# A decoder step with 64 experts: half of the expert pairs get their token rows from a 0/1 matmul, the others through VectorE turns, and the last pair is taken expert by expert

## The chip, the cores and the metric

The kernel runs on one core of one Trainium2 chip, in fp32. The metric is the device time of one execution in microseconds (us). Before the change three executions took 932.84, 932.85 and 930.03 us, a median of 932.84.

## The reference, cut to what matters

One inference step of a one-layer decoder for 256 prompt tokens and 8 sample tokens, model width 1024. A mixer (latent attention beside a state-space branch) comes first; the change does not touch its arithmetic. Then a mixture of experts:

```python
scores = sigmoid(t @ w_router)                 # t: 264 tokens x 1024, 64 experts in 8 groups
...                                            # the best 4 groups, in them the best 6 experts
combine = ...                                  # (264, 64): a token's weight for an expert, else 0
gte = einsum('td,edf->tef', t, w_gate_e)       # 64 experts, 1024 -> 256
upe = einsum('td,edf->tef', t, w_up_e)
routed = einsum('tef,efd->td', silu(gte) * upe * combine[:, :, None], w_down_e)
shared = (silu(t @ w_gate_s) * (t @ w_up_s)) @ w_down_s
out = x + g2 * rms_norm(routed + shared)
```

Each expert has 2 MiB of gate and up weights and 1 MiB of down weights, 192 MiB for all 64, and each weight is read once.

## The kernel before, in words

**Experts in pairs.** Experts are taken in 32 pairs q (experts 2q and 2q+1). For every pair a tile of 128 places is filled: four blocks of 32 places, one for each expert of the pair and each half of the prompt (l = 0: tokens 0 to 127, l = 1: tokens 128 to 255). In a block, LS = 28 places are for chosen prompt tokens and the last 4 hold sample tokens, which all experts compute. What does not fit into 28 places goes through a loop at the end (not entered with these inputs as long as no block overflows).

**Where the rows come from.** The normalised rows `h2` (two tiles of 128 tokens, also kept turned as `h2t`) are stored to DRAM as `tok_rows`. The router's choice is turned into a table `tab_g` of token numbers by four rounds of max and match_replace on VectorE (`take_lists`) and 8 small matmuls on TensorE (L2045). For each pair GpSimd issues `gather` (L1826), an indirect DMA from `tok_rows` into one of two buffers `xg`, and `gather_weights` (L1899), an indirect DMA of the routing weights into `wv` from `weight_tab`, a copy of the weights in DRAM (L1922). TensorE turns the 128 rows with 8 transposes (`turn_rows`, L2062), ScalarE copies them out of PSUM into `xt` (`rows_half`, L2331), and `xt` is the stationary operand of the expert's products.

**One pair on TensorE.** In this order: `gate_up(2q)`, `gate_up(2q+1)` (L2148, 32 instructions each; an fp32 product is two instructions); the two halves of `down_half(q-1, h)` (L2086), `turn_rows(q+1)`, `turn_inner(q)` (L2158, turns the inner activations), `combine` of pair q-1 (L2097, a matmul with a 128x128 weight matrix `wmat` that adds a pair's rows to the tokens' sums in PSUM banks 0 to 3). Between them ScalarE does the silu (L2342), VectorE multiplies gate and up (`hh`, L2571), makes `wmat` (L2535), copies the two halves of `down` out of PSUM (`half_out`, L2526), copies the turned inner activations (L2579) and adds the sample rows (`add_own`, L2562).

**Weights.** SyncE's queue loads gate/up weights into 6 slots and down weights into 6 slots. `load_gu(e)` waits until `gate_up(e-6)` is done; `load_dn(e)` waits until the pair's `down` before it in that slot is done. The down weights of the last two pairs come in two column halves (`load_dn_halves`, L1821). Expert 4's gate/up slot is the place of the shared expert's weights, so it is loaded in four parts, each when a part of the shared product is done (L1854); after the last of them the queue loads down weights 5 and 6 (L1814, L1861).

**The start of the stage.** TensorE does the last mixer product, the router (L1977) and the shared expert's gate and up products (`shared`, L1984), with the turns of `key` (L2033) and the table matmuls between them. The first `gate_up` starts after all of that.

**The end.** After `combine` of expert 63, ScalarE squares and VectorE scales the rows, each half when its sums are done; ScalarE loads the table for Sqrt once, at L2357, after its last silu. Then the rows are stored.

## Time and profile before

| | |
|---|---|
| median of the runs | 932.84 us |
| the profiled execution, its own time | 932.54 us |
| its span, first to last instruction | 930.8 us |
| PE busy | 870.0 us, 93% |
| DVE, ACT, POOL busy | 353.6, 194.6, 128.7 us |
| moved by DMA | 324.72 MB, mean 349 GB/s |

The span is cut into stretches below. In a row of windows the columns are: the stretch, its length, the busy time (and instructions) of PE, PEld, DVE, ACT and POOL, the granted TensorE clock as a share of full speed, the share of time in which the 16 DMA engines were busy, and the rate in GB/s. In a row of the timeline they are start, length, engine, line, operation, what is written and read, the shape, how many instructions are merged, and in brackets the idle time before it and what ended it. A row of groups ends with busy time, mean length of one instruction in ns, and idle time before them. The expert stage runs from about 453 us to 921 us.

### The profile page before, as it was taken

Reading aid. Unit: us, or ns where it says so; the run is one execution under the profiler, and the core shown is the slowest. Engines: PE = TensorE matmul, PEld = TensorE weight load, DVE = VectorE, ACT = ScalarE, POOL = GpSimd, SP = SyncE. Lnnn points to the kernel's source line nnn. Section 1 sums busy time; section 2 is a strip of 40 time slices with the busy share of each in tenths; the row PEclk is TensorE's granted clock in tenths of the full one; section 3 lists DMA queues with packets and bytes.
Section 4 is the critical chain, followed back from the end, with each engine's and each line's share of the span. In section 5 each row is a group of like instructions: output and inputs, shape, how many; then the busy total and the mean of one; then the engine's idle time right before and its main releaser. Section 6 shows DMA issues by size and latency. Waiting matters only on the chain.

```text
span 930.8 us, 18059 instructions
## 1 busy us (share of the span) xinstructions
PE 870.0 (93%) x7470; PEld 564.3 (61%) x7470; DVE 353.6 (38%) x800; ACT 194.6 (21%) x506; POOL 128.7 (14%) x155
## 2 busy tenths in 40 slices
PE   5999999997889899899899999999999998989897
PEld 3788888875666677657755555554555554545452
DVE  2315580037344689336223322322233222222225
ACT  2000110316222398033111111111111110101012
POOL 0000000022476000000302211101011110101100
PEclk9999999999999999999999999999999999999998
DMA  9966766727499939999999999999999999999993
GB/s 367 398 225 245 283 256 239 301 91 264 151 339 340 383 120 321 384 419 385 362 422 418 423 418 423 418 422 422 416 424 418 422 419 422 420 424 419 423 373 134
DMA packets 58564, 324.72 MB, mean 349 GB/s; under 512 B 13849, under 2 KB 22922, under 8 KB 37938
## 3 DMA queue, kind: packets, MB, share of 16 engines
q1 hardware_dynamic: 47154, 305.43, 81.8%
q0 software_dynamic: 9568, 17.93, 5.6%
q8 instruction: 61, 1.00, 0.4%
q10 hardware_dynamic: 1760, 0.20, 0.2%
q14 instruction: 21, 0.17, 0.1%
HBM read 326.55 MB, written 7.45 MB: 359 GB/s over the span
## 4 chain that ended last, share of the span: by engine, by line
PE 42%; DMA 17%; SPq 2%; DVE 2%; ACT 1%; issue 1%; POOLq 0%; DVEq 0%; ACTq 0%
PE bank L2148 17%; PE bank L2086 9%; PE bank L2097 4%; DMA slot_b<-in_w_e 4%; DMA x<-in_w_e 4%; DMA row_of<-in_w_e 4%; PE bank L1955 3%; PE bank L2062 2%; SPq L1806 1%; DMA ring<-in_w_units 1%; DMA out_ssm_s<-st 1%; DMA ac<-x_row 1%; PE bank L2158 1%; PE bank L2132 1%; SPq L1814 1%
## 5 line engine op out<-in xcount | busy, mean ns | idle before, releaser
L423 PE MATMUL bank<-h,ring 128*128 128x264 f32 x608 | 138.4, 388 | 0.5 <-PE bank L423 0.3
L423 PEld LDWEIGHTS bank<-h,ring 128*128 128x128 f32 x608 | 114.6, 190 | 21.9 <-issue 2.6
L2571 DVE TENSOR_TENSOR con<-scales_of,bank 64x256 f32<-64x256 f32 x64 | 27.2, 425 | 236.7 <-ACT scales_of L2342 236.7
L1826 POOL DMA_INDIRECT xg<-tok_rows,tab_g x32 | 36.1, 1129 | 364.4 <-PE bank L2062 315.1
L2086 PE MATMUL bank<-ring,ht 128*32 128x512 f32 x320 | 72.5, 595 | 10.1 <-DMA x<-in_w_e 5.2
L2342 ACT ACTIVATE scales_of<-bank 64x256 f32<-64x256 f32 x64 | 24.2, 378 | 274.0 <-PE bank L2148 274.0
L2148 PE MATMUL bank<-done_out,xt 128*64 128x256 f32 x704 | 78.4, 381 | 0.1
L2148 PE MATMUL bank<-ring,xt 128*64 128x256 f32 x672 | 77.2, 382 | 0.4 <-ACT xt L2331 0.4
L2526 DVE COPY sq<-bank 128x512 f32<-128x512 f32 x64 | 44.3, 692 | 73.5 <-PE bank L2086 73.5
L2148 PEld LDWEIGHTS bank<-done_out,xt 128*64 128x64 f32 x704 | 50.5, 137 | 30.1 <-issue 7.0
L2148 PEld LDWEIGHTS bank<-ring,xt 128*64 128x64 f32 x672 | 46.8, 137 | 35.0 <-issue 14.1
L2097 PE MATMUL bank<-sq,con 64*128 64x512 f32 x256 | 65.6, 609 | 0.0
L2331 ACT COPY xt<-bank 128x448 f32<-128x448 f32 x64 | 31.0, 532 | 134.3 <-PE bank L2062 134.3
L2086 PEld LDWEIGHTS bank<-ring,ht 128*32 128x32 f32 x320 | 18.2, 109 | 52.8 <-issue 52.8
L2062 PEld LDWEIGHTS bank<-con,xg 128*128 128x128 f32 x256 | 27.4, 140 | 27.5 <-issue 27.5
L637 POOL DMA_DIRECT2D page<-in_cache x20 | 12.0, 601 | 231.6 <-issue 224.3
L2086 PE MATMUL bank<-done_out,ht 128*32 128x512 f32 x176 | 39.9, 595 | 4.4 <-DMA row_of<-in_w_e 4.4
L2148 PE MATMUL bank<-slot_b,xt 128*64 128x256 f32 x352 | 39.9, 379 | 0.8 <-DMA slot_b<-in_w_e 0.8
L2086 PE MATMUL bank<-slot_b,ht 128*32 128x512 f32 x176 | 39.9, 595 | 0.0
L2086 PE MATMUL bank<-row_of,ht 128*32 128x512 f32 x176 | 39.9, 595 | 0.0
L2562 DVE SCALAR_TENSOR_TENSOR acc<-sq,own_w,acc 128x1024 f32<-128x1024 f32 x30 | 38.3, 1275 | 0.0
L2062 PE MATMUL bank<-con,xg 128*128 128x128 f32 x256 | 34.9, 279 | 1.8 <-DVE con L2571 1.0
(471 smaller groups left out, 1281.2 us busy)
## 6 DMA issues: line engine op xcount, KB each, us to landing
ring<-in_w_units SPq DMA_DIRECT2D x25, 2048.0 KB, 11.4
done_out<-in_w_e SPq DMA_DIRECT2D x22, 2048.0 KB, 29.5
ring<-in_w_e SPq DMA_DIRECT2D x20, 2048.0 KB, 28.7
slot_b<-in_w_e SPq DMA_DIRECT2D x11, 2048.0 KB, 30.5
slot_f<-in_w_e SPq DMA_DIRECT2D x10, 2048.0 KB, 29.8
ring<-in_w_e SPq DMA_DIRECT2D x19, 1024.0 KB, 30.8
slot_b<-in_w_e SPq DMA_DIRECT2D x10, 1024.0 KB, 30.2
done_out<-in_w_e SPq DMA_DIRECT2D x10, 1024.0 KB, 28.7
```

Source lines behind the costliest of these rows:

```text
L423: mm = pe.matmul(bank[:, t % NB, 0:T], w[:, j, k, :], h[:, k, :], start=(k == 0), stop=(k == KD - 1))
L1826: pool.indirect_dma_start(xg[q % AHEAD][:, :], None, tok_rows, bass.IndirectOffsetOnAxis(ap=tab_g[:, q:q + 1].bitcast(U32), axis=0), bound ...
L1955: mm = pe.matmul(bank[:, 2 * j + h, :], merged[:, k, j * P:(j + 1) * P], w_out[:, k, part_of(h)], start=(k == 0), stop=(k == KD - 1))
L2062: mm = pe.transpose(bank[:, 5 + h, i * P:(i + 1) * P], xg[q % AHEAD][:, k * P:(k + 1) * P], ident)
L2086: mm = pe.matmul(bank[lo:lo + HB, 6 + h, :], ht[q % 2][:, e % 2 * 2 + k, l * HB:(l + 1) * HB], down_at(e)[:, k, h * 512:(h + 1) * 512], st ...
L2097: mm = pe.matmul(bank[:, 2 * l + h, :], wmat[q % 2][at, :], yo[q % NYO][at, h * 512:(h + 1) * 512], start=(q == 0), stop=(q == NPAIR - 1))
L2148: mm = pe.matmul(bank[c * LB:(c + 1) * LB, 4 + e % 2, 0:FE], xt[:, k, e % 2 * LB:(e % 2 + 1) * LB], gu_w[e % SLOTS][:, k, c * FE:(c + 1) * ...
L2331: act.copy(xt[:, KD // 2 * h:KD // 2 * (h + 1), :].rearrange("p k (x s) -> p k x s", s=HB)[:, :, :, 0:LS], bank[:, 5 + h, :].rearrange("p ...
L2342: act.activation(sg[e % 2][:, :], bank[0:LB, 4 + e % 2, 0:FE], ACT.Silu).then_inc(sg_ready, 1)
L2526: dve.tensor_copy(yo[q % NYO][:, h * 512:(h + 1) * 512], bank[:, 6 + h, :]).then_inc(y_ready, 1)
L2562: ins = dve.scalar_tensor_tensor(acc[:, :], yo[q % NYO], own_w[:, q:q + 1], acc[:, :], ALU.mult, ALU.add)
L2571: dve.tensor_tensor(hh[e % 2][:, :], sg[e % 2][:, :], bank[LB:2 * LB, 4 + e % 2, 0:FE], ALU.mult).then_inc(hh_ready, 1)
```

## The change

1. `gather` serves only every second pair of pairs (q mod 4 = 2 or 3, called fetched), into a single buffer `xg`. GpSimd issues them in its loop: for q mod 4 = 0 after the weights of q the rows of q+2, for q mod 4 = 2 ahead of the weights of q the rows of q+1. VectorE turns them (`turn_rows`): for each expert of the pair 8 transposes of 32 partitions x 256 elements straight from `xg` into `xt`.
2. For q mod 4 = 0 or 1, four experts at a time (a group, EG = 4), TensorE forms `xt` with `burst`: 16 matmuls of `h2` (128x128, stationary) with a 0/1 matrix `sel` (128 x 4x28 columns), which selects and turns at once; ScalarE copies four results (`take_rows`). `sel` comes from a count of chosen tokens ahead of each (a matmul with `before`, `pos_done`), `places` and `select` on VectorE. `h2` now has a place of its own.
3. `half_out` moves from VectorE to ScalarE.
4. The start: the bursts of group 0, the two `pos` matmuls and 8 transposes of the sample rows come before the second half of the shared products; the lists (`keys_of`, `take_lists`) and the table matmuls come after them. The sample rows go into `xg` by four small DMAs.
5. Gate/up weights of expert 5: the last 2560 of 4096 columns are loaded in the mixer's last phase, the rest as before.
6. The end: only the last pair's down weights come in column halves; expert 63's gate/up weights come last but these, in two halves; TensorE does `gate_up(62)`, `down` and `combine` of pair 30, and then `gate_up(63)`.

```diff
@@ the mixer's last phase, SyncE
                         load_row(0)
                         load_row(1)
+                        sp.dma_start(slot_f[:, EARLY_GU:GU], io["w_e"][5][:, EARLY_GU:GU]
+                                     ).then_inc(small_in, 16)
                         sp.wait_ge(y_done6, 2)
@@ SyncE, expert stage
-                        sp.wait_ge(own_in, 1)
+                        sp.wait_ge(own_cols, 2)
                         load_dn(sp, 5)
-                        sp.wait_ge(rows_stored, 32)
+                        sp.wait_ge(wgt_ready, 1)
                         sp.dma_start(w_sd[:, :, :].rearrange("p k c -> p (k c)"), io["w_e"][EXTRA][:, GU:EW]).then_inc(w_sd_in, 16)
                         for e in range(NE):
-                            if e + SLOTS < NE:
+                            last = e + SLOTS == NE - 1
+                            if e + SLOTS < NE and not last:
                                 load_gu(sp, e + SLOTS)
-                            if e % 2 and 3 <= e < NE - 7:
+                            if e % 2 and 3 <= e < NE - 5:
                                 for n in (e + 3, e + 4):
-                                    if EXTRA < n < NE - 4:
+                                    if EXTRA < n < NE - 2:
                                         load_dn(sp, n)
+                            if last:
+                                sp.wait_ge(gu_done, e + 1)
+                                for h in range(2):
+                                    part = slice(h * GU // 2, (h + 1) * GU // 2)
+                                    sp.dma_start(gu_at[(NE - 1) % SLOTS][:, part], io["w_e"][NE - 1][:, part]).then_inc((gu_in[(NE - 1) % SLOTS], last_gu_in)[h], 16)
                             if e == NE - 6:
-                                load_dn_halves(sp, NE - 4)
-                            if e == NE - 5:
                                 load_dn_halves(sp, NE - 2)
@@ GpSimd
+                        pool.wait_ge(srow_took, 1)
+                        for x4 in range(4):
+                            pool.dma_start(xg[x4 * HB + LS:(x4 + 1) * HB, :], rows_s[x4 % 2 * OWN:x4 % 2 * OWN + OWN, :]).then_inc(own_in, 16)
                         pool.wait_ge(wgt_ready, 1)
                         for a, lo in ((0, 0), (2, P)):
                             pool.dma_start(weight_tab[lo * NE:(lo + P) * NE, :].rearrange("(t e) o -> t (e o)", e=NE),
                                            wgt[:, a, :]).then_inc(tab_stored, 16)
-                        gather(pool, AHEAD)
+                        pool.wait_ge(own_in, 16 * 4)
+                        pool.wait_ge(rows_stored, 32)
                         pool.wait_ge(tab_stored, 32)
-                        gather_weights(0)
-                        gather_weights(1)
-                        gather(pool, AHEAD + 1)
-                        for q in range(2, NPAIR):
-                            if q + AHEAD < NPAIR:
-                                gather(pool, q + AHEAD)
+                        for q in range(NPAIR):
+                            if q % 4 == 2:
+                                gather(pool, q + 1)
                             gather_weights(q)
+                            if q % 4 == 0:
+                                gather(pool, q + 2)
@@ TensorE
+                        def burst(n, i):
+                            l, ks = i // 2, range(KD // 2 * (i % 2), KD // 2 * (i % 2 + 1))
+                            ...
+                            for k in ks:
+                                at = k % (KD // 2) * P
+                                out = bank[:, b, at:at + P].rearrange("p (e s) -> p e s", e=EG)[:, :, 0:LS]
+                                mm = pe.matmul(out, h2[:, l, k * P:(k + 1) * P], sel[:, l, :, :], start=True, stop=True)
+                            mm.then_inc(xt_done, 1)
@@ TensorE, start of the stage (order after the change)
                         shared(0, 0, 0, P)
                         shared(0, 0, P, T - P, low)
+                        pe.wait_ge(chosen_ready, 1)
+                        pe.matmul(bank[:, 1, 0:NE], ccol("before"), chosen[:, 0, :], start=True, stop=True).then_inc(pos_done, 1)
+                        shared(0, 0, P, T - P, high).then_inc(sgu_done, 1)
+                        shared(1, 0, 0, P, high)
+                        ...                                  # the same for chosen[:, 2, :]
+                        shared(1, 0, P, T - P).then_inc(sgu_done, 1)
+                        for i in range(4):
+                            burst(0, i)
                         ...                                  # key turns, shared(0, 1), shared(1, 1) first part, table matmuls
@@ TensorE, loop
-                            if q + 1 < NPAIR:
-                                for h in range(2):
-                                    turn_rows(q + 1, h)
-                            turn_inner(q)
+                            if q % 4 == 3 and q + 1 < NPAIR:
+                                for i in range(4):
+                                    burst((q + 1) // 4, i)
+                            if q < NPAIR - 1:
+                                turn_inner(q)
@@ VectorE
-                        def half_out(n):
+                        def turn_rows(q, h):
+                            if h == 0:
+                                dve.wait_ge(x_in, 16 * (nth_fetched(q) + 1))
+                            dve.wait_ge(gu_done, 2 * q - 3 + h)
+                            for l in range(2):
+                                at = h * LB + l * HB
+                                rows = xg[at:at + HB, :].rearrange("p (k r c) -> p r k c", k=KD, r=4)
+                                for r in range(4):
+                                    ins = dve.transpose(xt[32 * r:32 * r + 32, :, 2 * q % EG + h, l, :], rows[:, r, :, :])
+                            ins.then_inc(turned_ready, 1)
                         for q in range(NPAIR):
                             for e in (2 * q, 2 * q + 1):
+                                if e == NE - 1:
+                                    weight_matrix(q - 1)
                                 ...                          # wait for the silu, multiply: hh
+                                if q % 4 == 1 and e % 2 == 0:
+                                    turn_rows(q + 1, 1)
+                                if q % 4 == 2:
+                                    turn_rows(q + 1, e % 2)
-                            if q:
+                            if q and q < NPAIR - 1:
                                 weight_matrix(q - 1)
-                                half_out(2 * q - 2)
-                                half_out(2 * q - 1)
                             ...                              # wait for turn_inner, copy ht, add_own(q - 1)
+                            if q % 4 == 0:
+                                turn_rows(q + 2, 0)
+                            if q % 4 == 1 and q + 3 < NPAIR:
+                                dve.wait_ge(xt_done, q + 3)
+                                select(slice(0, 2), q // 2 + 2).then_inc(sel_ready, 1)
                             if q == 0:
                                 own_weights()
```

TensorE waits at q = 1, between the two halves of `down` of pair 0, for what `own_weights` writes; that wait is in both kernels.

## Rows read from the trace of the kernel before

**Rows 1.** Windows: whole core, five stretches.
```profile
344.00:348.00 4.00, 4.00 (x53) 3.52 (x52) 2.12 (x3) 3.97 (x14) 0.00 (x0) 1.00 0.00 0
448.00:452.00 4.00, 3.24 (x29) 3.07 (x28) 0.43 (x1) 0.00 (x0) 0.36 (x1) 1.00 0.77 263
500.00:550.00 50.00, 50.00 (x440) 26.54 (x434) 16.17 (x27) 6.14 (x14) 10.69 (x8) 1.00 1.01 421
...
913.00:916.00 3.00, 3.00 (x27) 1.25 (x20) 1.97 (x4) 0.00 (x0) 0.00 (x0) 1.00 0.16 59
916.00:919.00 3.00, 3.00 (x28) 0.81 (x28) 1.60 (x4) 0.00 (x0) 0.00 (x0) 1.00 0.06 16
```

**Rows 2.** The chain that ended last: turns, a shared product, one pair, waits, the end.
```profile
474.21 1.02 PE bank L2062 x8
...
630.76 3.63 PE bank L2132 x8
...
707.09 7.06 PE bank L2148 x64
714.14 3.57 PE bank L2086 x32
717.71 1.02 PE bank L2062 x8
718.74 0.33 PE bank L2158 x3
719.07 1.83 PE bank L2097 x8
...
796.08 37.95 DMA row_of<-in_w_e
...
858.18 38.60 DMA x<-in_w_e
...
921.32 0.70 DVE slot_b L2665
```

**Rows 3.** DMA issues, 880 to 931 us, and SyncE's timeline: the last halves.
```profile
row_of<-in_w_e SPq DMA_DIRECT2D x2, 512.0 KB, 11.1
...
906.08 1.16 SPq L1821 DMA_DIRECT2D row_of<-in_w_e  x1
```

**Rows 4.** Timeline of TensorE at the start of the stage.
```profile
443.31 0.33 PE L2045 MATMUL bank<-con,listed_p 128*32 128x32 f32 x16 [0.95 <-DVE listed_p L2475]
443.57 7.55 PE L1984 MATMUL bank<-x,ring 128*128 128x128 f32 x64
451.88 1.07 PE L2062 MATMUL bank<-con,xg 128*128 128x128 f32 x8 [0.76 <-DMA xg<-tok_rows,tab_g]
453.30 3.03 PE L2148 MATMUL bank<-ring,xt 128*64 128x256 f32 x26 [0.35 <-ACT xt L2331]
```

**Rows 5.** DMA queues, 500 to 700 us: packets, MB, share of 16 engines.
```profile
q0 software_dynamic: 2386, 2.80, 4.0%
```

**Rows 6.** VectorE's timeline: the last step of the routing weights.
```profile
446.27 0.58 DVE L2511 TENSOR_SCALAR wgt<-wgt,need 128x64 f32<-128x64 f32 x3
```

**Rows 7.** GpSimd's timeline: a gather behind the turns that free its buffer.
```profile
476.00 0.99 POOL L1826 DMA_INDIRECT xg<-tok_rows,tab_g  x1 [11.73 <-PE bank L2062]
```

**Rows 8.** DMA issues, 445 to 470 us: size, median us to landing.
```profile
weight_tab<-wgt POOLq DMA_DIRECT2D x2, 32.0 KB, 5.1
```

**Rows 9.** The gathers (L1826): landing after issue, min, median, max.
```profile
DMA to landing us min/median/max: 6.9/10.4/11.6
```

**Rows 10.** Groups of VectorE by shape; the last is from the mixer.
```profile
L2571 DVE TENSOR_TENSOR con<-scales_of,bank 64x256 f32<-64x256 f32 x61 | 25.9, 425 | 223.6 <-ACT scales_of L2342 223.6
L2535 DVE TENSOR_SCALAR con<-mod,tok_f,wv 128x128 f32<-128x128 f32 x30 | 10.2, 339 | 0.0
...
L501 DVE TENSOR_SCALAR h<-sq,scales_of,mod 128x256 f32<-128x256 f32 x8 | 2.9, 410 | 0.1
```

**Rows 11.** ScalarE's timeline: the table for Sqrt.
```profile
911.36 1.28 ACT L2357 ACT_TABLE_LOAD   x1
```

More of the change, by code:

```diff
@@ L75 @@
 SPREAD = 4
+EG = 4
 TAKEN, SENT = -3e38, 3e38
@@ L2015, in _ @@
                         turn_half(0, 1)
+                        pe.wait_ge(x1_ready, 2)
+                        for k in range(KD):
+                            mm = pe.transpose(bank[0:TS, k // 4, k % 4 * P:(k % 4 + 1) * P], h2t[:, k, TP:T], ident)
+                        mm.then_inc(srow_done, 1)
                         pe.wait_ge(score_ready, 2)
@@ L2161, in _ @@
                         pe.wait_ge(fresh, 1)
[L2162 to L2163 removed]
                         for q in range(NPAIR):
[L2165 to L2166 removed]
+                            gate_up(2 * q)
+                            if q < NPAIR - 1:
+                                gate_up(2 * q + 1)
                             if q:
@@ L2197, in _ @@
                                 more = overflow(pe)
+                        gate_up(NE - 1)
+                        turn_inner(NPAIR - 1)
                         for h in range(2):
@@ L2493, in _ @@
                         route(2, 2, 3)
+                        for l, a in ((0, 0), (1, 2)):
+                            places(l, a)
+                            select(slice(l, l + 1), 0).then_inc(sel_ready, 1)
+                        keys_of(0)
+                        keys_of(2)
                         take_lists()
```

266 lines of the change are left out of this document (151 added, 115 removed).

## The prediction, made blind

> **What bounds the kernel now.** I read the page first (PE busy 93%), then the windows, then the chain of waits, and last the timelines around the start and the end of the expert stage. The page alone misleads. In the expert stage TensorE is busy without a gap at 500 to 550 us, but the DMA share is 1.01 at 421 GB/s in the same stretch [rows 1]: two resources are full at once. The chain says which of them ends last. A pair costs TensorE 7.06 (gate and up) + 3.57 (down) + 1.02 (turn of the rows) + 0.33 (turn of the inner activations) + 1.83 (combine) = 13.81 us, and up to about 730 us the chain is nothing but this pattern. Behind it come waits for down weights that were issued 38 us earlier: they land at 796.08 + 37.95 = 834.0 and 858.18 + 38.60 = 896.8, four pairs apart, which is 15.7 us a pair [rows 2]. So TensorE (13.8) is faster than the DMA (15.7); it eats the six prefetched experts up to 730 us and then waits. The stage is bound by DMA from its start: 201 MB of expert weights, plus what else is in the queues. After 896.8 the chain is pure TensorE until 921.3, when VectorE begins the final rows; the very last weights land at 906.08 + 11.1 = 917.2 [rows 2, 3].
>
> There is one hole in the DMA: 0.77 at 448 to 452 [rows 1]. By then every free slot is filled, and what SyncE has left (a quarter of expert 4, down weights 5 and 6) waits for the last shared product, which ends at 443.57 + 7.55 = 451.1 [rows 4]. Everything after this point is one full queue of work, so the last landing moves with (a) the time at which that product ends and (b) the bytes behind it. A saving on TensorE by itself is worth nothing.
>
> **The change, part by part.** The sum is made against the profiled execution's 932.54 us (span 930.8), which is 0.3 us under the median of 932.84.
>
> *Start, TensorE.* Ahead of the last shared product come the bursts of group 0: 16 matmuls, two instructions each. The nearest price is the shared product's 7.55/64 = 0.118 us with the same 128x128 stationary operand and 128 columns [rows 4]; the burst has 112 columns. 32 x 0.118 = 3.8. The two counts add 4 instructions, 0.5. The wait of 0.95 for the lists [rows 4] goes: the lists now run beside half of the shared product (32 instructions, 3.8 us). The 8 sample-row turns cost between 0 and 0.9; I take 0.1, for ScalarE's copies are waited for there anyway. Net 3.4: the last shared product ends at 454.5. The first gate_up can start at once, where before 0.76 + 1.07 + 0.35 lay between [rows 4], so it starts at 454.5 instead of 453.3.
>
> *Start, DMA.* SyncE's last quarter, down 5 and 6 move by the same +3.4. The 1.31 MB of expert 5 that now go out at 344 to 348, where the DMA stands at 0.00 [rows 1], cost nothing there, and bring nothing either: they are taken from the stretch ahead of the hole and only make the hole 3.1 us longer. What would be hidden is hidden already.
>
> *Fewer gathers.* q0 takes 4.0% of 200 us = 8.0 us for the 200/13.81 = 14.5 pairs of that stretch, 0.55 a pair, nearly all of it the rows (2.80 MB) [rows 5]. As a mean over engines a gather is then worth 0.5. But the last landing is that of the most laden engine: after 913 us only 16% and 6% of the engines still work, for some 4 to 5 us [rows 1]. Spread over 30 gathers that is 0.15 more each. I take 0.63, bounds 0.5 and 0.8. Before, 30 gathers lay behind the hole (the first two in it), now 16: 14 x 0.63 = -8.8 (7.0 to 11.2).
>
> *Early stall.* This is the part that the change adds unawares. Routing weights: tables at 452.5, then 443.57 to 446.85, 3.3 us, as before [rows 4, 6]: 455.8. GpSimd wakes 0.8 us later, as behind the turns that end at 474.21 + 1.02 = 475.2 [rows 2], whose gather starts at 476.0 [rows 7], and stores the weights in two issues: landed at 5.1 [rows 8] plus about 2 for the fuller queues (a gather lands in 6.9 at the least and 10.4 at the median [rows 9]), 464.5. Then the weights of pair 0 (1.3), and only then the rows of pair 2 at 466, landing 10.4 later [rows 9]: 476.4. VectorE's instruction that waits for them stands ahead of own_weights, and TensorE, done with gates 0 to 3 and half a down at 472.5, waits for that. A turn for one expert is 8 transposes of 256 elements. No transpose is in the trace; the nearest are VectorE instructions of 256 elements a partition, mean 410 ns, but 8 of them busy 2.9 us in pairs, so that the second of a pair adds 0.33 [rows 10]. I take 0.33, 2.67 a turn; bounds 0.28 and 0.45 (no overlap at all). Own weights at 479.6, the next multiply (0.43), a turn, a multiply: combine of pair 0 ends near 485.5. The rows of pair 3 are issued when that turn has freed the only buffer (482.7 + 0.8 + 10.4 = 493.9) and are followed by turn, multiply, turn, wmat (0.34) [rows 10]: 500.0. TensorE reaches gate_up(6) at 501.8, some 10 us later than before. The slots freed late leave the DMA queues dry two or three times by about half a us: +1.5 (0 to 6).
>
> *Steady state, TensorE.* Without turns 12.79 a pair, a burst (3.8) every fourth: 54.96 per four instead of 55.24. No gain, and none needed. VectorE gives up half_out and gains 42.7 us of turns; it stays under half busy. But at q mod 4 = 2 it does turn, multiply, turn, wmat in a row behind a gather that was issued only when the turn before it was done. Counted from the start of q = 4: that turn ends at 20.0, rows at 20.0 + 0.8 + 10.4 = 31.2, wmat at 37.3; TensorE would like it at 36.5. So 0.75 of stall for each of 7 such pairs, 5.2 in all.
>
> *TensorE's own path.* 501.8 + 16.6 (q = 3 with burst) + 27 x 12.79 + 6 x 3.8 + two shared products (3.63 each [rows 2]) + 1.5 of small ones + 5.2 = 900.6 for gate_up(62).
>
> *DMA's path.* Last landing 917.2 + 3.4 + 1.5 - 8.8 - 0.3 (half as many narrow packets) = 913.0. Behind the down weights of expert 61 lie 4.2 MB, 10.2 us, so those land at 902.8.
>
> *End.* From 902.8: down 3.57, combine 1.83, gate_up(63) 3.53, silu and multiply 1.0, turn 0.33, copy 0.5, down 3.57, first combine 1.0: 918.1. TensorE's path gives 900.6 + 3.53 + the same 15.3 = 919.4. The split transfers are then not what ends last; expert 63's serial chain is. I take 918.8 against 921.3: -2.5. Last, half_out of expert 63 on ScalarE now stands ahead of the table load of 1.28 us, which before lay 10 us ahead of the end [rows 11]: the first square comes 1.0 later. Sum: 932.54 - 2.5 + 1.0 = 931.0.
>
> **A rule that speaks against it.** By the Trainium skill, "VectorE: DVE Perf Modes", section "The DRAIN you can't avoid", the next VectorE instruction does not start before the pipe of the last is empty; by this a turn would be 8 full lengths. The rows of 256 elements show an overlap instead (8 x 0.41 = 3.3, busy 2.9), so the trace agrees with this rule of the Trainium skill only in part. The same page of the Trainium skill, section "The three transpose paths", has 311 ns for a 128x128 bf16 turn; my estimate from it, with 128 more elements at one a cycle of 0.96 GHz, is 0.44 us an instruction; the sum by either would be that of the second rival below.
>
> **The rivals.**
>
> *The stall is hidden.* Landing under 10 us or turns of 0.30, so that VectorE is in time, gathers worth 0.7 or more: the DMA path alone with 14 x 0.75 and no early idle. Last landing 910, end 915.3, time 927.5. For it: the DMA share is 1.01 everywhere behind the hole. Against it: 10.4 is the median.
>
> *VectorE becomes the bound (slower).* Per group three turns are in the loop, 24 transposes; each 0.1 us more in one is 2.4 us per group, 17 over seven. TensorE's path has nothing to spare, so that it decides from about 0.36 us an instruction. At 0.42 (as the mean of 0.41 without overlap [rows 10]): gate_up(62) at 900.6 + 15 + 2, end 936, time 950; at 0.38, 940. Against it: single-source instructions overlap in pairs here.
>
> *The start costs more.* Weight table and rows of pair 2 land 3 us later than I took, or the chains of selects hold the bursts: both paths +4, time 935.
>
> *The change doesn't do what it says:* a block that overflows in one way of filling and not in the other would show in the loop at the end; the same 28 places are filled, so I give it nothing.
>
> **How the numbers follow.** Likeliest (0.50): both paths near each other, 931.0, own range 927.5 to 934.5. Hidden stall 0.20, VectorE as the bound 0.20, costlier start 0.10. A difference of 0.3%, 2.8 us, is what a measurement of this kernel can tell: below 930.0 is faster, above 935.6 slower. Faster: 0.24 of the first case and all of the second, 0.44. Slower: all of VectorE's case, 0.04 of the costlier start and 0.02 of the first, 0.26. Same 0.30. Range 925.5 to 941.
>
> **What would show it.** Right: the last shared product ends near 454.5; TensorE idles 5 to 8 us at L2086 or its like in pair 0's down, near 472 to 480, for own_weights; q0's share in the stage falls to nearly half; transposes 0.33 us apart; waits for down weights come late, after 850, and are short; the table load stands behind the last copies. Wrong: DMA share clearly under 1 after 500 us, waits of TensorE for w_ready in every fourth pair of more than 1 us, or a last landing after 917.

## The result: 3.4% slower

The changed kernel takes 962.84 us (median of 6, 960.72 to 965.01), the kernel before 931.37 us (median of 6); ratio 1.0341, 95% interval 1.0322 to 1.0360. The forecast was 931.0 us with a range up to 941; the time lies outside it, above even the figure that the rival "VectorE becomes the bound" gave for 0.42 us a transpose (950).

Profile after, by groups (line, engine, operation, out<-in, shape, count | busy us, mean ns | idle before it and what ended it); the last two rows are transfers of expert weights (count, size, median us from issue to landing):

```profile
L2617 DVE STREAM_TRANSPOSE xt<-xg 32x256 f32<-32x256 f32 x256 | 111.5, 436 | 29.1 <-DMA xg<-tok_rows,tab_g 25.4
L2137 PE MATMUL bank<-sq,con 64*128 64x512 f32 x256 | 76.4, 706 | 23.0 <-DVE con L2627 23.0
...
done_out<-in_w_e SPq DMA_DIRECT2D x21, 2048.0 KB, 11.4
slot_f<-in_w_e SPq DMA_DIRECT2D x9, 2048.0 KB, 10.3
```

A "turn" here is the 8 transposes of one expert's rows on VectorE; "the matrix" is `wmat`, the weights that `combine` multiplies by. A transpose lasts 436 ns, where the forecast took 330 for each. TensorE's combine (L2137) waits 23.0 us in all for the matrix from VectorE (L2627), which stands behind the turns. The expert weights now land some 9 to 13 us after their issue (medians of the tiles, 500 to 900 us), where before they took up to 38 [rows 2]: the queues are no longer backlogged. None of TensorE's waits after 440 us is for weights, so the DMA has ceased to be what sets the pace. The busy share hides this, for it hardly fell. The same 400 us before and after, us, busy time and count of PE, PEld, DVE, ACT, POOL; PE's granted clock; DMA share; GB/s:

```profile
500.00:900.00 400.00, 384.73 (x3212) 204.87 (x3208) 112.89 (x193) 46.55 (x108) 58.11 (x54) 1.00 1.01 419
500.00:900.00 400.00, 376.98 (x3058) 199.86 (x3056) 157.16 (x336) 63.38 (x129) 43.17 (x39) 0.96 0.99 411
```

VectorE at q mod 4 = 2, once in every group of four pairs (start, us, instruction, count, idle before it):

```profile
739.42 3.58 DVE L2617 STREAM_TRANSPOSE xt<-xg 32x256 f32<-32x256 f32 x8 [3.03 <-DMA xg<-tok_rows,tab_g]
743.03 0.42 DVE L2663 TENSOR_TENSOR con<-scales_of,bank 64x256 f32<-64x256 f32 x1
743.48 3.59 DVE L2617 STREAM_TRANSPOSE xt<-xg 32x256 f32<-32x256 f32 x8
747.11 0.35 DVE L2627 TENSOR_SCALAR con<-mod,tok_f,wv 128x128 f32<-128x128 f32 x1
```

A turn is 3.58 / 8 = 0.447 us from start to start: each transpose waits for the whole of the one before. TensorE at the same time:

```profile
743.51 0.46 PE L2203 MATMUL bank<-con 64*128 64x64 f32 x4 [0.98 <-DVE con L2663]
747.60 3.78 PE L2137 MATMUL bank<-sq,con 64*128 64x512 f32 x8 [3.63 <-DVE con L2627]
751.32 7.31 PE L2193 MATMUL bank<-done_out,xt 128*64 128x256 f32 x64
```

It waits 0.98 us for the multiply behind the first turn, 3.63 us for the matrix behind the second, and then the combine takes 3.78 us where it took 1.83 [rows 2]. The windows, in the same columns as above, say why:

```profile
744.00:748.00 4.00, 0.40 (x2) 0.43 (x4) 3.85 (x10) 0.00 (x0) 0.00 (x0) 0.61 0.94 401
748.00:750.00 2.00, 2.00 (x6) 0.83 (x6) 1.10 (x1) 0.00 (x0) 1.75 (x1) 0.50 1.11 475
750.00:752.00 2.00, 2.00 (x10) 0.45 (x8) 0.00 (x0) 0.00 (x0) 0.00 (x0) 0.57 0.92 393
752.00:756.00 4.00, 4.00 (x40) 2.64 (x38) 0.37 (x1) 0.38 (x1) 0.00 (x0) 1.00 1.01 414
```

Granted clock 0.50 is 1.2 GHz, the lower of its two levels; TensorE had been busy for 0.40 of the four us before. And in the chain of work that ended last the loop can be followed round (start, us, what):

```profile
781.90 3.63 PE bank L2193 x32
...
785.96 0.42 DVE con L2663
...
786.42 0.43 DVE xt L2617
...
790.78 11.43 DMA xg<-tok_rows,tab_g
...
802.23 0.43 DVE xt L2617
...
809.92 0.36 DVE con L2627
...
810.42 3.79 PE bank L2137 x8
```

These are the first gate_up of q mod 4 = 1, its multiply (after ScalarE's silu, left out here), a turn (which frees the one buffer), the next gather of 11.4 us, a turn, a multiply, a turn, the matrix, and the late combine. From the multiply to the matrix's end it is 24.3 us (785.96 to 810.28), and TensorE has work for 19.8 of them:

```profile
785.96:810.28 24.32, 19.82 (x172) 9.42 (x168) 14.70 (x33) 3.47 (x7) 1.99 (x2) 0.99 1.01 425
```

From one late combine to the next, seven groups of four pairs take 433.1 us (498.62 to 931.72), 61.9 in the mean and 59.5 to 62.8 where no shared product lies between. In the version below whose turns are on TensorE, which hardly waits, a group takes 57.0 (a gate_up at 799.16, the same of the next group at 856.12).

### The profile page after: what moved, and what is told of

Same layout as the page of the kernel before. It is cut to its first block, busy times and chain, and to the rows that moved or that the text cites. A ratio compares the mean times of both kernels' runs of the same rounds, so it can differ in the third digit from the quotient of the medians.

```text
span 963.4 us, 18257 instructions
## 1 busy us (share of the span) xinstructions
PE 885.8 (92%) x7482; PEld 568.3 (59%) x7482; DVE 423.8 (44%) x1002; ACT 218.7 (23%) x539; POOL 115.2 (12%) x140
## 4 chain that ended last, share of the span: by engine, by line
PE 39%; DMA 8%; DVE 8%; issue 3%; ACT 0%; POOL 0%; POOLq 0%; DVEq 0%
PE bank L2193 16%; DMA xg<-tok_rows,tab_g 8%; PE bank L2126 7%; PE bank L2137 6%; DVE xt L2617 6%; PE bank L2017 3%; PE bank L1976 3%; PE bank L2024 1%; DVE con L2663 1%; PE bank L2172 1%; PE bank L2203 1%; DMA weight_tab<-wgt 0%; DVE con L2627 0%; PE bank L2032 0%; PE bank L1998 0%
## 5 line engine op out<-in xcount | busy, mean ns | idle before, releaser
L2617 DVE STREAM_TRANSPOSE xt<-xg 32x256 f32<-32x256 f32 x256 | 111.5, 436 | 29.1 <-DMA xg<-tok_rows,tab_g 25.4
L2137 PE MATMUL bank<-sq,con 64*128 64x512 f32 x256 | 76.4, 706 | 23.0 <-DVE con L2627 23.0
L2126 PE MATMUL bank<-ring,ht 128*32 128x512 f32 x320 | 74.5, 607 | 6.9 <-DVE own_w L2644 6.9
L2193 PE MATMUL bank<-ring,xt 128*64 128x256 f32 x672 | 79.4, 390 | 0.0
L1923 POOL DMA_INDIRECT wv<-weight_tab,tok_i x32 | 38.0, 1186 | 318.1 <-DVE con L2627 266.5
L2395 ACT COPY sq<-bank 128x512 f32<-128x512 f32 x64 | 37.4, 585 | 94.9 <-PE bank L2126 94.9
L2137 PEld LDWEIGHTS bank<-sq,con 64*128 64x128 f32 x256 | 29.3, 213 | 41.7 <-issue 40.8
L2673 DVE COPY ht<-bank 128x256 f32<-128x256 f32 x32 | 13.6, 424 | 83.8 <-PE bank L2203 83.6
## 6 DMA issues: line engine op xcount, KB each, us to landing
done_out<-in_w_e SPq DMA_DIRECT2D x21, 2048.0 KB, 11.4
```

The lines of the kernel that those rows point to most:

```text
L1923: pool.indirect_dma_start(wv[:, q:q + 1], None, weight_tab, bass.IndirectOffsetOnAxis(ap=tab_w[:, q:q + 1].bitcast(U32), axis=0), bounds_c ...
L2126: mm = pe.matmul(bank[lo:lo + HB, 6 + h, :], ht[q % 2][:, e % 2 * 2 + k, l * HB:(l + 1) * HB], down_at(e)[:, k, h * 512:(h + 1) * 512], st ...
L2137: mm = pe.matmul(bank[:, 2 * l + h, :], wmat[q % 2][at, :], yo[q % NYO][at, h * 512:(h + 1) * 512], start=(q == 0), stop=(q == NPAIR - 1))
L2193: mm = pe.matmul(bank[c * LB:(c + 1) * LB, 4 + e % 2, 0:FE], xt[:, k, e % EG, :, :].rearrange("p l n -> p (l n)"), gu_w[e % SLOTS][:, k, c ...
L2395: act.copy(yo[q % NYO][:, h * 512:(h + 1) * 512], bank[:, 6 + h, :]).then_inc(y_ready, 1)
L2617: ins = dve.transpose(xt[32 * r:32 * r + 32, :, 2 * q % EG + h, l, :], rows[:, r, :, :])
```

## The experiments

Ratios are to the kernel before, run on the same chip; its medians there were 930.2 to 931.1 us. All edits are to the changed kernel unless said. Versions that leave out transposes, or put copies or other rows in their place, compute another product; they are there for their time.

### Fewer transposes a turn: 4, 6, 7

The first edit shortens a turn and leaves everything else in place.

```
-                                for r in range(4):
+                                for r in range(3):        # turns6; 2 in turns4; 4 if l else 3 in turns7
```

> The changed kernel with 6 of the 8 transposes of each turn (a quarter of the fetched rows is not turned, so those experts work on old columns). A turn then takes 6 x 0.447 = 2.7 us, which is what the prediction took for a whole turn. Theory (a transpose is priced wrong, the rest of the prediction holds): 931 to 936. Rival A (something else in the change costs the 30 us: the selecting matmuls, the copies on ScalarE, the order at the end): 950 or more, at most 10 us regained. Rival B (a stall also lowers TensorE's clock, so that the loss is more than the loop's excess): the gain per group is more than 6 x 0.447 = 2.7 us, and granted clock returns to 1.00 in the stage.

> 4 of the 8 transposes of each turn (half of the fetched rows not turned), a turn of 1.8 us. Theory: VectorE is out of the path and the DMA or TensorE's plain sum sets the time, 927 to 932, at most 4 us under the kernel with 6. Rival A (the turns are not it): over 945. If the loss were in proportion to the transposes all the way (no threshold), this would be as far under the kernel with 6 as that is under the changed one.

> The changed kernel with 7 of the 8 transposes of each turn (an eighth of the fetched rows is not turned): a turn of 3.13 us, as if a transpose took 0.39. By the formula of the prediction's rival (VectorE in the path from 0.36 us a transpose on, 2.4 us per group for each 0.1 us) 943. If the step from 6 to 8 transposes (930 to 963) is even, 946. If it sets in only between 7 and 8: under 935.

| transposes a turn | us a turn | median us | ratio, 95% interval |
|---|---|---|---|
| 4 | 1.8 | 928.85 | 0.9981 (0.9957 to 1.0004) |
| 6 | 2.7 | 930.21 | 1.0011 (0.9991 to 1.0031) |
| 7 | 3.1 | 946.91 | 1.0174 (1.0148 to 1.0199) |
| 8 | 3.6 | 962.84 | 1.0341 (1.0322 to 1.0360) |

With a turn of the length that the forecast took, the whole rest of the change costs what the forecast said: 930.2 against 931.0. That it agrees to 1 us is partly luck, as terms of the sum were off in both directions (below). But nothing else in the change makes it slow. Between 4 and 6 almost nothing happens (1.4 us), from 6 on each further transpose costs 16 to 17 us: a threshold, where the loop on VectorE becomes longer than TensorE's work. In the kernel with 6, TensorE's wait for the matrix is 1.45, 1.83 and 1.38 us in the first three groups and 0.16 to 0.86 from then on (7.3 in all, where the changed kernel has 23.0), and no late combine is slowed:

```profile
553.31 1.99 PE L2137 MATMUL bank<-sq,con 64*128 64x512 f32 x8 [1.83 <-DVE con L2627]
672.93 1.99 PE L2137 MATMUL bank<-sq,con 64*128 64x512 f32 x8 [0.16 <-DVE con L2627]
```

### The turns of the fetched pairs on TensorE (pe_turns)

TensorE turns the fetched rows and ScalarE copies them into `xt`, as before the change; all else stays.

```
+    for i in range(KD // 2):                     # PE: behind the down halves, banks 5 and 6, as before the change
+        k = KD // 2 * h + i
+        mm = pe.transpose(bank[:, 5 + h, i * P:(i + 1) * P], xg[:, k * P:(k + 1) * P], ident)
...
+    act.copy(xt[:, KD // 2 * h:KD // 2 * (h + 1), at:at + 2, :, 0:LS].rearrange("p k e l s -> p k (e l) s"),      # ACT
+             bank[:, 5 + h, :].rearrange("p (k x s) -> p k x s", x=4, s=HB)[:, :, :, 0:LS])
...
-    ins = dve.transpose(xt[32 * r:32 * r + 32, :, 2 * q % EG + h, l, :], rows[:, r, :, :])
```

> The changed kernel with the fetched pairs' rows turned by TensorE (8 transposes, 1.02 us a pair) and copied by ScalarE, as before the change; all else stays. TensorE's sum for four pairs becomes 4 x 12.79 + 3.8 + 2 x 1.02 = 57.0 against 55.2 before, still under the DMA's 4 x 15.7 less two gathers. Theory (VectorE's turns alone cost the time; the rest of the change is worth a little): 927 to 932. Rival A (the rest costs too): 935 to 950. Rival C (TensorE is now the bound): 932 to 936, with waits for down weights gone from the chain.

931.16 us (928.16 to 936.88), ratio 1.0019 (0.9989 to 1.0049): the loss is gone as far as can be measured, with the same number of gathers and bursts. The theory's time holds. So does the half of rival C that speaks of the profile, that TensorE is now the bound: in the profiled execution TensorE waited 2.6 us in all between 440 and 920 us (who waited for what, us in total, times, longest), and no weights are among it:

```profile
PE bank L2215 <- DVE con L2676: 1.9, 2, 0.9
PE bank L2138 <- DVE ht L2682: 0.5, 1, 0.5
PE bank L2029 <- DMA xg<-tok_rows,tab_g: 0.2, 1, 0.2
```

### A second buffer for the fetched rows (twobuf)

The rows of pairs with q mod 4 = 3 go into a place of their own (half of `h2`, whose other half the later bursts then read twice), so their gather need not wait for a turn.

```
-                pool.indirect_dma_start(xg[:, :], None, tok_rows,
+                pool.indirect_dma_start((xg[:, :], h2[:, 1, :])[q % 2], None, tok_rows,
-                    pool.wait_ge(turned_ready, 2 * nth_fetched(q))
+                    pool.wait_ge(turned_ready, 2 * nth_fetched(q) - 2)     # for the third fetched pair and on
```

> The changed kernel with all 8 transposes of 0.44 us a turn, but with a second buffer for the rows of the pairs with q mod 4 = 3, so that their gather does not wait for the turns of the pair before and lands early. (The buffer is the second half of h2; the bursts behind group 0 read its first half twice, and the sample rows are not put into it, so those values are other than the reference's.) Theory (what costs is the loop turn, gather of 10 to 11 us, turn, turn, matrix on a single buffer; VectorE's busy time is under half): VectorE starts the turns right behind its multiplies, a turn of 3.6 us still makes the second multiply and the matrix up to 1.3 us late, time 928 to 936. Rival (the turns' busy time itself, ahead of the multiplies in the queue of VectorE, is the cost): over 945.

936.78 us (934.91 to 942.09), ratio 1.0068 (1.0047 to 1.0088). All 8 transposes at full length are in it, and 26 of the 31 us are gone: busy time on VectorE by itself costs at most what is left. The rest is the loop that the single buffer closes: a gather of 11 us that can't start before a turn has ended, with two turns behind it. In what is left TensorE waits 12.5 us for the matrix, 1.6 at the most, which still stands behind the second turn:

```profile
PE bank L2140 <- DVE con L2630: 12.5, 8, 1.6
```

### TensorE kept busy in the hole (warm)

Needless matmuls, whose result is overwritten, fill the time in which TensorE waits for the matrix.

```
                            if q < NPAIR - 1:
                                turn_inner(q)
+                           if q % 4 == 2:
+                               for _ in range(4):
+                                   pe.matmul(bank[:, 5, :], ident, h2[:, 0, 0:512], start=True, stop=True)
```

> The changed kernel with 4 extra matmuls (128x512, about 0.9 us each) in the hole ahead of the late combine of every fourth pair (q mod 4 = 2); their result is overwritten. In the changed kernel that combine waits 3.63 us (743.97 to 747.60), the granted clock then stands at 0.50 to 0.57 until 752, the combine takes 3.78 us instead of 1.83 and the next gate_up 7.31 instead of 7.06, 2.2 us per group. Theory (the idle time itself lowers TensorE's clock, and the loss of 32 us is 7 stalls of 4.6 us beside 7 times 2.2 us of slow matmuls): combine back at 1.83, clock 1.00 behind it, 948 (10 to 16 us faster than the changed kernel). Rival (the clock falls for another reason, or the combine is slow for its operands): combine stays near 3.8, time 962 or more.

957.20 us (954.92 to 958.30), ratio 1.0268 (1.0237 to 1.0300). Adding 3.7 us of needless matmuls to every fourth pair makes the kernel 5.6 us faster (6.8 by the two ratios). The sign shows the clock's part, and so do the rows of the same place:

```profile
742.22 3.70 PE L2229 MATMUL bank<-h,con 128*128 128x512 f32 x8
745.92 1.99 PE L2137 MATMUL bank<-sq,con 64*128 64x512 f32 x8
```
```profile
744.00:748.00 4.00, 4.00 (x15) 1.51 (x15) 3.32 (x7) 0.00 (x0) 1.46 (x1) 1.00 1.01 430
```

Clock 1.00, combine 1.99 us. The same group shrinks from 62.8 us (late combines at 747.60 and 810.42) to 60.7 (745.92 and 806.63), by 2.1, as expected (2.2). The gain in all was expected too large (10 to 16 us) for two reasons that the rows show. Two of the changed kernel's seven groups end in a combine that was not slowed, so there was little to regain:

```profile
687.78 1.99 PE L2137 MATMUL bank<-sq,con 64*128 64x512 f32 x8 [1.57 <-DVE con L2627]
```

And the first late combine comes 2.7 us later (501.36, not 498.62), for there the needless matmuls are longer than the hole. Seven groups take 423.7 us instead of 433.1, 9.4 less, and with the later start 6.7 are left.

### own_weights ahead of the first turn (own_early)

```
+                            if q == 0:
+                                own_weights()
                             if q % 4 == 0:
                                 turn_rows(q + 2, 0)
```

> The changed kernel with own_weights ahead of the first turn of pair 2, so that TensorE does not wait 6.9 us for it in pair 0's down. Theory (the loop gather, turn, turn, gather, turn, turn on VectorE sets the pace, and TensorE waits for the weights of pair 2 or the rows of pair 3 instead): the wait moves, the time stays within 2 us of the changed kernel's 962.8. Rival (the early wait is on the path by itself and everything shifts with it): 6 to 7 us faster, 956.

964.19 us (961.16 to 964.74), ratio 1.0362 (1.0333 to 1.0392): no gain. The early wait of 6.9 us, which the forecast had found, only moves to TensorE's next instruction that needs something from behind the turns:

```profile
485.93 0.58 PE L2203 MATMUL bank<-con 64*128 64x64 f32 x3 [10.47 <-DVE con L2663]
```

### Why the transposes do not overlap (one_quadrant, copies, copies_one_quadrant)

```
-   ins = dve.transpose(xt[32 * r:32 * r + 32, :, 2 * q % EG + h, l, :], rows[:, r, :, :])
+   ins = dve.transpose(xt[32 * (2 * h + l):32 * (2 * h + l) + 32, :, 2 * q % EG + r // 2, r % 2, :], rows[:, r, :, :])   # one_quadrant
# copies: dve.tensor_copy in the first line; copies_one_quadrant: dve.tensor_copy in the second
```

In the two versions whose output stays, an expert's rows are spread over both turns of a pair, so gate_up waits for both turns and the first turn for one gate_up more; this changes when a turn may start, not what is in it.

> The changed kernel with the same 8 transposes of 32x256 a turn, but the 4 that read one group of 32 partitions also write one and the same group (each to other columns), where the changed kernel writes another group of 32 partitions each time. The rows land in other places, so the product is other than the reference's. Theory Q (a VectorE instruction that starts its input or output in another group of 32 partitions than the one before it is held until that has ended; the rows of 256 elements from which the prediction took 0.33 us all stay in one group): 6 of 8 transposes start about 0.35 us after the one before, a turn takes 0.35 x 6 + 0.44 x 2 = 3.0 us and the time falls to 938 to 944. Theory T (a transpose never overlaps with the next): starts stay 0.447 apart, 962.

> The changed kernel with plain copies of the same 32x256 elements, from and to the same partitions, in the place of the transposes (the rows aren't turned, so the product is other than the reference's). Theory Q: held all the same, starts a full copy (0.41 to 0.42) apart, a turn of 3.4 us, time 952 to 960. Theory T: copies overlap, starts 0.33 apart, a turn of 2.7 us, 930 to 932.

> Both edits: plain copies, and 4 in a row that write the group of 32 partitions of their input group. Theory Q and theory T: starts 0.33 apart within the four, a turn of 2.7 to 2.9 us, 930 to 937. If starts stay a full length apart here too, what makes the rows of the prediction overlap is something else.

| | output moves to another 32 partitions each time | four in a row stay |
|---|---|---|
| transposes | turn 3.58 us, 962.84 us | turn 2.84 us, 937.90 us, ratio 1.0072 (1.0049 to 1.0096) |
| copies | turn 2.36 us, 928.80 us, ratio 0.9976 (0.9956 to 0.9996) | turn 1.78 us, 927.97 us, ratio 0.9975 (0.9954 to 0.9996) |

VectorE with the four staying in one group of 32 partitions, then copies that move, then copies that stay:

```profile
727.64 2.84 DVE L2617 STREAM_TRANSPOSE xt<-xg 32x256 f32<-32x256 f32 x8 [2.29 <-DMA xg<-tok_rows,tab_g]
```
```profile
526.60 2.36 DVE L2617 COPY xt<-xg 32x256 f32<-32x256 f32 x8
```
```profile
525.71 1.78 DVE L2617 COPY xt<-xg 32x256 f32<-32x256 f32 x8
```

Theory Q holds in both rows of the table: staying in the group saves 0.74 us a turn of transposes and 0.58 of copies, where only the output's partitions (and the columns there) differ. The transposes of the turn at 727.64 start at 727.64, 728.00, 728.33 and 728.66, so 0.33 to 0.36 apart within the four, and the next four, which read and write another group, start at 729.06, 0.40 later. That is near the 0.33 of the forecast. For copies that stay, 1.78 - 0.28 - 0.29 over six is 0.20 apart, and copies that move start 2.36 / 8 = 0.295 apart, their full length. So what decides whether they overlap is the change of partitions, and not the transposing; the transposing makes the single instruction longer (0.436 us against 0.284). The median transpose of the version that stays also lasts less, 0.394 us. The time expected for the copies that move was wrong under theory Q (952 to 960), as a copy of this size is shorter in itself (0.28 us, not 0.41), and a turn of 2.36 us is below the threshold, held or not. By the Trainium skill, "VectorE: DVE Perf Modes", section "Two Vector instructions with no wait between them", an instruction is held until all earlier VectorE instructions have ended if an input of it starts in another quadrant (group of 32 partitions) than the first input of the last instruction that read that memory, or its output in another than the last output there; these runs agree with it (0.447 us apart held, 0.33 to 0.36 not). A correct turn of such transposes can't profit from it (argued from the layout, not run): it must bring each of the four groups of rows into each of the four groups of features, so that no two of a pair's 16 transposes have both input and output group in common.

### Parts of the change alone (pe_turns_noend, pe_late_f)

Both start from the kernel with its turns on TensorE. In the first, gate_up(62) and gate_up(63) stand together again and expert 63's weights come whole; in the second, expert 5's weights come in one transfer behind h2_ready.

```
-                            if q < NPAIR - 1:
-                                gate_up(2 * q + 1)
+                            gate_up(2 * q + 1)                       # pe_turns_noend
-                        sp.dma_start(slot_f[:, EARLY_GU:GU], io["w_e"][5][:, EARLY_GU:GU]).then_inc(small_in, 16)
+                        load_gu(sp, 5)                               # pe_late_f, at its old place
```

> The kernel with all turns on TensorE, without the change's last part: the last pair's two gate_ups stand together again and expert 63's gate and up weights come in one transfer. Theory (TensorE is the bound there, the weights are in time, and with expert 63 alone at the end its chain gate_up 3.6, silu 0.4, multiply 0.4, turn 0.5, copy 0.4 is the same as with both experts together, while the down of pair 30 is put between): 0 to 2 us slower without the part, as the down of pair 30 then no longer hides the silu of expert 62. Rival (the part is worth what it was made for, the wait for the last weights): 3 us or more slower.

> The kernel with all turns on TensorE, with expert 5's weights loaded in one piece behind h2_ready as before the change, not 1.3 MB of them at 344 us. Theory (the early piece only makes the hole in the DMA at 443 to 455 us longer; TensorE is the bound behind it): no difference, within 1 us. Rival (the early bytes are gained): 3 us slower without it.

931.09 us (ratio 1.0008, 0.9992 to 1.0024) and 931.93 us (ratio 1.0013, 0.9997 to 1.0030), against 931.16 with both parts: neither can be told from nothing. The last transfers are not what ends last in the version with its turns on TensorE, whose DMA stands still from 908 us on (below), and the bytes brought forward only leave the DMA idle later. In a kernel whose DMA sets the pace either part may be worth something; no run here shows it.

### Versions meant to be faster (mixed, mixed_tail, mixed2)

The turns are shared between the two engines; the lines show which pairs' rows each engine turns.

```
 mixed:       VectorE turns pairs with q mod 4 = 2 (a pair early), TensorE those with q mod 4 = 3; own_weights first
+    if q % 4 == 2:                                                   # PE
+        for h in range(2): turn_rows(q + 1, h)
-                                if q % 4 == 2:                       # DVE
-                                    turn_rows(q + 1, e % 2)
 mixed_tail:  and the last pair's two half_outs on VectorE
 mixed2:      mixed, with pair 2 turned by TensorE too
+    if q % 4 == 2 or q == 1:
```

> A version meant to be faster than both: the rows of pairs with q mod 4 = 2 turned by VectorE (a pair early, so in nobody's way), those of q mod 4 = 3 by TensorE (1.02 us) with copies on ScalarE, own_weights ahead of the first turn. TensorE's sum for four pairs is 4 x 12.79 + 3.8 + 1.0 = 56.0 against 57.0 of the kernel with all turns on TensorE. Theory (that one was bound by TensorE over its whole stage, its chain shows no DMA): 7 us less if DMA allows it, and DMA's last landing then sets 926 to 929. Rival (DMA was as late as TensorE): 929 to 931, no difference from the kernel with all turns on TensorE.

> The last version with the two half_outs of the last pair on VectorE instead of ScalarE, so that ScalarE's table load of 1.28 us does not stand behind them. Theory: 1.0 to 1.5 us faster than the last version. Rival (hidden behind the combine of the first half): no difference.

> As the mixed version, but the rows of pair 2 are turned by TensorE too, so that VectorE has no wait for a gather ahead of the multiplies of pair 1 (in the mixed version TensorE waited 11.2 us for that). VectorE turns the rows of the pairs 6, 10, ... 30 only. Theory (the kernel with all turns on TensorE was bound by TensorE from 500 us on, and its DMA was done 12 us before the DMA of the kernel before): TensorE saves 7 x 1.02 = 7 us, time 922 to 926. Rival (the DMA is then as late, or something of the end is fixed): 928 to 931.

mixed took 931.86 us (ratio 1.0003, 0.9986 to 1.0020), near the rival's number, but with a wait that neither side had named. VectorE stands in front of the gather of pair 2 with the multiplies of pair 1 queued behind it:

```profile
481.73 0.58 PE L2219 MATMUL bank<-con 64*128 64x64 f32 x3 [11.21 <-DVE con L2691]
```

mixed_tail took 932.88 us (1.0015, 0.9994 to 1.0035): no gain, so moving the last copies from in front of the table load regains nothing that can be measured. mixed2 takes the wait of 11.2 us away: 926.97 us (924.55 to 935.53), ratio 0.9975 (0.9960 to 0.9990). It is faster than the kernel before by 0.25% (2.3 us; 3.5 in the medians), a third to a half of the 7 that TensorE was to save, and the fastest version here that leaves nothing out. In its profiled execution, the slowest of the 13 (935.53 us), the DMA is what holds TensorE back: it waits 3.5 us for down weights, and one transfer of 38 us is in the chain that ended last. How much of that the median has isn't known.

```profile
PE bank L2140 <- DMA row_of<-in_w_e: 2.3, 1, 2.3
858.82 38.25 DMA x<-in_w_e
```

## Why the prediction was wrong

**The step that failed** is the price in "No transpose is in the trace; the nearest are VectorE instructions of 256 elements a partition [...] I take 0.33, 2.67 a turn". Measured: 0.447 us from start to start, 3.58 a turn. The bounds were 0.28 to 0.45, so it lay at the very end of them, and the rows chosen as nearest [rows 10] differed in what decides: they stayed in the same partitions, the transposes move. The forecast's own words on the Trainium skill's rule of no overlap said that the trace agreed "only in part"; for these instructions it agrees in full, and the estimate of 0.44 an instruction that stood beside it was right.

**The mechanism was foreseen**, and is the second rival's: VectorE in the loop turn, gather, turn, multiply, turn, matrix, deciding from about 0.36 us a transpose on. Measured is a threshold between 6 x 0.447 / 8 = 0.335 and 7 x 0.447 / 8 = 0.391. It was given 0.20, and the range ended at 941, short of the 950 that the rival's own text gives for 0.42 us (by its own terms 948), though 0.45 was within the bounds of the price.

**The rival's price was too low.** By its formula 0.447 - 0.33 = 0.117 on 24 transposes is 2.8 us a group. From the version with 6 transposes to the changed kernel, gate_up(6) comes 4.7 us later (497.71 and 502.43) and gate_up(62) 34.7 (899.05 and 933.71), so 30.0 us over seven groups, 4.3 a group. TensorE's longer waits for VectorE (21.3 us for the matrix instead of 5.9, and 3.3 more for the multiplies) are 2.7 of it, near the rival's price. The late combines (22.5 us for the seven instead of 13.9, as five of them take 3.5 to 3.8 instead of 1.99) are 1.2 more. The last 0.4 are not accounted for. The forecast had no term for the clock, though PE's clock is a column of the windows that it read; there it stands at 1.00 in all five.

**What held** (the forecast in brackets). A burst takes 3.75 us (3.8). Own weights are written at 477.2 (479.6), with TensorE's wait of 6.9 us in pair 0's down (7.1). The rows of pair 3 landed at 490.4 (493.9), gate_up(6) began at 502.4 (501.8). The agreement of this last one is luck: rows that landed 3.5 us early made up for two turns 0.9 us longer each and a slow combine (3.30 us). In the kernel with 6 transposes gate_up(62) came at 899.05 (900.6), and the whole took 930.2 (931.0). Of the signs of being wrong, the waits for the matrix in every fourth pair and the late last landing (the DMA was still 0.47 busy at 920 to 930 us) showed; a DMA share clearly under 1 did not (0.99). The early piece of expert 5 was worth nothing (0), and the hole in the DMA grew: 0.31 and 0.33 of the engines busy at 443 to 453 us, where [rows 1] have 0.77 at 448 to 452.

```profile
443.00:448.00 5.00, 5.00 (x43) 4.64 (x43) 2.75 (x14) 2.74 (x4) 0.00 (x0) 1.00 0.31 125
448.00:453.00 5.00, 5.00 (x58) 4.56 (x58) 2.21 (x11) 0.39 (x1) 0.00 (x0) 1.00 0.33 108
```

**What was off beside it.** VectorE's gain was put at 42.7 us of turns, which is 16 turns of 2.67; there are 32, two for each of the 16 fetched pairs, so 85.4 by its own price and 111.5 measured. The sum did not use this figure, and VectorE still stayed at 44%. The start was costed 2 us too dear (gate_up(0) at 452.45, forecast 454.5), and the weight table landed at 459.2, not 464.5. The DMA was done somewhat earlier than forecast: with 6 transposes it runs dry at 908 to 912, and with the turns on TensorE by 908, where the sum had 913.0. The smaller start is some 2 us of that; the gathers may be worth a little more than 8.8 us, which no run shows by itself:

```profile
908.00:912.00 4.00, 3.75 (x34) 2.21 (x32) 0.00 (x0) 0.20 (x1) 0.00 (x0) 1.00 0.21 79
```
```profile
900.00:908.00 8.00, 8.00 (x66) 3.27 (x66) 0.68 (x2) 1.55 (x3) 0.00 (x0) 1.00 0.45 167
908.00:916.00 8.00, 6.55 (x54) 2.50 (x52) 2.56 (x6) 2.10 (x4) 0.00 (x0) 1.00 0.00 0
```

It did not turn into time: TensorE's own path, with 3.8 for a burst in place of four turns' 4.1, had nothing to give. The split end was worth nothing either. The table load does stand behind the last copies as forecast (952.63 us, 1.28 long, in the chain of the changed kernel), but its +1.0 could not be regained by taking them off ScalarE. The forecast's total for these small terms, -1.5, was within what can't be told apart from zero; the 0.3% that it named itself are 2.8 us.

## What to carry to other kernels

Before work is moved to an engine that is "under half busy", draw the loop that it closes: here a single buffer, a transfer of 11 us that waits for its release, and everything queued behind on that engine. The busy share says nothing of it, and past the point where the loop is as long as the other engine's work, each 0.45 us a turn cost 16 us in all. When an operation is not in the trace, look for the nearest row by what its instructions touch (which partitions, one after the other), not by its element count alone; and when the two ends of such a price lie on both sides of a threshold, the far end deserves as much weight as the near one.

## What the runs showed of the hardware that was not expected

- VectorE, 32x256 f32 from SBUF to SBUF: a transpose takes 0.436 us and starts 0.447 apart when its output moves to another group of 32 partitions; when input and output stay they start 0.33 to 0.36 apart. A copy takes 0.28 and starts 0.295 and 0.20 apart.
- TensorE after a wait: behind 3.63 us of idle time with 0.98 shortly before, the granted clock was 0.50 and the same combine took 3.78 us instead of 1.83. Needless matmuls in the hole kept it at 1.00. By the Trainium skill, "TensorE: Matmul & The Clock Gate", section "What's actually happening", an idle array falls back to 1.2 GHz and has to be busy again before it is given 2.4; the trace agrees (0.50 at 748 to 750 us, 1.00 again from 752). The length of the last wait alone does not tell whether the clock falls. In the changed kernel a wait of 1.69 us was followed by a slow combine and one of 1.57 (above) was not; in the version with 7 transposes a wait of 2.13 was, and one of 3.02 was not:

```profile
498.62 3.30 PE L2137 MATMUL bank<-sq,con 64*128 64x512 f32 x8 [1.69 <-DVE con L2627]
859.59 3.65 PE L2137 MATMUL bank<-sq,con 64*128 64x512 f32 x8 [2.13 <-DVE con L2627]
557.39 1.99 PE L2137 MATMUL bank<-sq,con 64*128 64x512 f32 x8 [3.02 <-DVE con L2627]
```

- The gathers hardly gained by shorter queues: the weights landed after 9 to 13 us instead of up to 38, but the gathers on the chain (790.78 above) still took 11.4, and the median of all 16 is 10.1, against 10.4 before [rows 9].
